# Four places of 4 MB for the expert weights, each matrix in two transfers

## The reference, cut to what matters

```
x = layer_norm(ALPHA * x + token_mixer(x), ln1_g, ln1_b)      # ends in merged @ w_out
logits = x @ router_w + router_b                              # 32 experts, top 4, softmax
for each expert e, for the tokens xb sent to it:
    gt = min(xb @ w_gate[e] + b_gate[e], 7)
    up = clip(xb @ w_up[e] + b_up[e], -7, 7)
    y  = (gt * sigmoid(1.702 * gt) * (up + 1)) @ w_down[e] + b_down[e]
out = layer_norm(ALPHA * x + sum of gate * y over a token's experts, ln2_g, ln2_b)
```

## Time and profile before

| | before |
|---|---|
| median of the runs | 2550.3 us |
| span of the profiled execution | 2550.5 us |
| TensorE busy | 2339.3 us (92%) |
| read from memory | 601.03 MB |
| transfers: queue of the kernel, share of 16 engines | 60.2% |

### The profile page before, as it was taken

The page is one execution under the profiler, slowest core; times in us unless marked ns, Lnnn a source line. Parts: engine busy times, 40 slices in busy tenths (PEclk is TensorE's granted clock), DMA queues, the critical chain, the costliest instruction groups (busy, mean ns, idle before and its releaser), DMA issues.

```text
span 2550.5 us, 32955 instructions
## 1 busy us (share of the span) xinstructions
PE 2339.3 (92%) x13502; PEld 1575.8 (62%) x13502; DVE 970.7 (38%) x1582; ACT 821.9 (32%) x1253; POOL 61.7 (2%) x34
## 2 busy tenths in 40 slices
PE   6989889999999977779999889999999999999996
PEld 4944777886888977679889788333333334333332
DVE  5466444343342486666654655211111111111112
ACT  4367433232242454635534673111111111111101
POOL 0000000000000023200000000000000000000000
PEclk8999999999999988889999999999999999999998
DMA  9287054432221300225546144999999999999995
GB/s 341 72 294 229 1 181 134 131 99 99 83 99 67 132 1 1 100 67 187 178 181 231 67 116 191 396 430 433 430 430 428 429 432 420 432 429 422 427 418 228
DMA packets 133298, 603.71 MB, mean 237 GB/s; under 512 B 5728, under 2 KB 51040, under 8 KB 116672
## 3 DMA queue, kind: packets, MB, share of 16 engines
q1 hardware_dynamic: 133184, 602.10, 60.2%
HBM read 601.03 MB, written 1.05 MB: 236 GB/s over the span
## 4 chain that ended last, share of the span: by engine, by line
PE 74%; DMA 11%; ACT 7%; DVE 5%; issue 2%; SPq 0%; ACTq 0%; DVEq 0%
PE bank L994 73%; DMA arena<-in_b_up 10%; ACT arena L1906 1%; DMA ring<-in_ada_w 1%; ACT modp L1681 1%; ACT w_high L2115 0%; ACT arena L2275 0%; ACT arena L2184 0%; ACT wide_p L2172 0%; ACT w_split L1747 0%; PE bank L1219 0%; PE bank L1589 0%; DVE arena L2745 0%; DVE last_sums L2684 0%; DMA ring<-in_ffn_w_up 0%
## 5 line engine op out<-in xcount | busy, mean ns | idle before, releaser
L994 PE MATMUL bank<-arena 128*64 128x512 f32 (+6 forms) x2264 | 447.2, 501 | 92.5 <-ACTq L782 29.0
L994 PEld LDWEIGHTS bank<-arena 128*64 128x64 f32 (+2 forms) x2264 | 207.3, 166 | 280.3 <-issue 194.1
L994 PE MATMUL bank<-hT_high,w_split 128*128 128x512 f32 (+1 forms) x1408 | 346.6, 337 | 2.5 <-DVE hT_low L2346 2.4
L994 PE MATMUL bank<-ring,arena 128*64 128x512 f32 (+1 forms) x1120 | 267.8, 593 | 2.1 <-ACT arena L2262 1.0
L994 PEld LDWEIGHTS bank<-hT_high,w_split 128*128 128x128 f32 x1408 | 242.1, 190 | 31.4 <-issue 2.8
L994 PE MATMUL bank<-up_w,arena 128*64 128x512 f32 x1024 | 233.6, 609 | 19.2 <-DMA arena<-in_b_up 19.1
L994 PE MATMUL bank<-hT_low,w_split 128*128 128x512 f32 (+1 forms) x704 | 236.6, 336 | 0.0
L3022 DVE TENSOR_SCALAR arena<-bank 128x512 f32<-128x512 f32 x32 | 22.1, 691 | 550.3 <-PE bank L994 550.0
L994 PEld LDWEIGHTS bank<-ring,arena 128*64 128x64 f32 (+1 forms) x1120 | 100.8, 141 | 162.7 <-issue 152.5
L994 PEld LDWEIGHTS bank<-up_w,arena 128*64 128x64 f32 x1024 | 78.8, 140 | 172.7 <-issue 172.7
L994 PEld LDWEIGHTS bank<-hT_low,w_split 128*128 128x128 f32 x704 | 133.6, 190 | 14.5 <-issue 1.0
(11 more groups left out here) (422 smaller groups left out, 4060.2 us busy)
## 6 DMA issues: line engine op xcount, KB each, us to landing
ring<-in_w_gate SPq DMA_DIRECT2D x32, 4096.0 KB
up_w<-in_w_up SPq DMA_DIRECT2D x32, 4096.0 KB
arena<-in_w_down SPq DMA_DIRECT2D x64, 2048.0 KB, 14.7
ring<-in_ada_w SPq DMA_DIRECT2D x24, 2048.0 KB, 8.7
ring<-in_ffn_w_up SPq DMA_DIRECT2D x44, 1024.0 KB, 7.7
ring<-in_w_in SPq DMA_DIRECT2D x11, 2048.0 KB, 8.0
ring<-in_ffn_w_down SPq DMA_DIRECT2D x10, 2048.0 KB, 7.7
ring<-in_hgrn_w_in SPq DMA_DIRECT2D x10, 2048.0 KB, 7.9
```

What stands on the lines that cost most here:

```text
L994: return pe.matmul(o, l, r, start=start, stop=stop)
```

## The change

- Four places of 4 MB: ring slots 1 and 2; the first two units of the arena; ring slot 0 with a further unit of the arena; and a new one over memory that is free after the router (half of `xr`, `hT`, half of `gb`). Matrix n goes to place n mod 4. The gate of expert e now waits for the down product of expert e-2 (gd_ready at e-1), the up for the gate product of expert e-1, the down for the up product of e-1.
- Each matrix goes as two transfers of 2 MB with a semaphore each for expert parity and half; TensorE waits for the second half only before k = 4. Gate and up halves are 16 KB out of every 32 KB for a partition.
- The first half of gate 0 is issued when ring slot 1 is free, the second at slot 2, up's halves after mixed_out(0,1) and (1,1), down 0 at once, gate 1 after the router's sums.
- Biases have two places. The bodies of TensorE's loop (two pairs) and SyncE's loop (four experts) are longer.
- The last `combine` stands ahead of the branch and closes the sums tile by tile; the further pass adds its own sums.
- The array `wide` is moved and worked in two halves.

```diff
-        moe_slot = [ring[:, i, :] for i in range(RING)] + [region(i * UNIT, UNIT) for i in range(6 - RING)]
+        freed_w = nc.alloc_sbuf_tensor_at("freed_w", [P, 2, UNIT], F32, offset=xr_at + 4 * XT * D)
+        moe_unit = [(ring[:, 1, :], ring[:, 2, :]), (region(0, UNIT), region(UNIT, UNIT)),
+                    (ring[:, 0, :], region(2 * UNIT, UNIT)), (freed_w[:, 0, :], freed_w[:, 1, :])]
+        WIDE = (ITEMS + 2) // 2
...
-        def expert_units(sp, e, i, first=False):
+        def expert_half(sp, name, e, buffer, j, landed):
+            w = a[name][0][bass.ds(e, 1)]
+            if name == "w_down_2":
+                src = w.rearrange("e (j p c) n -> p (e j) (c n)", j=2, p=P)[:, j, :]
+            else:
+                src = w.rearrange("e (p j c) n -> p (e j) (c n)", j=2, p=P)[:, j, :]
+            sp.dma_start(moe_unit[buffer][j], src).then_inc(landed[j], 16)
...
+        def first_experts(sp):
+            sp.wait_ge(SEM[owner[1][0]], owner[1][1])
+            expert_half(sp, "w_gate_2", 0, 0, 0, gate_landed[0])
+            expert_bias(sp, "b_gate_2", 0, 0, 0, gate_landed)
+            expert_bias(sp, "b_up_2", 0, 32, 0, up_landed)
+            sp.wait_ge(SEM[owner[2][0]], owner[2][1])
+            expert_half(sp, "w_gate_2", 0, 0, 1, gate_landed[0])
+            sp.wait_ge(psum_ready, group[("wo2", 0, 1)] + 1)
+            expert_half(sp, "w_up_2", 0, 1, 0, up_landed[0])
+            sp.wait_ge(psum_ready, group[("wo2", 1, 1)] + 1)
+            expert_half(sp, "w_up_2", 0, 1, 1, up_landed[0])
+            expert_weights(sp, "w_down_2", 0, 2, down_landed[0])
+            sp.wait_ge(psum_ready, group[("route",)] + 1)
+            expert_weights(sp, "w_gate_2", 1, 3, gate_landed[1])
...
+            sp.wait_ge(gg_ready, 1)
+            expert_weights(sp, "w_up_2", 1, 0, up_landed[1])
+            sp.wait_ge(gu_ready, 1)
+            expert_weights(sp, "w_down_2", 1, 1, down_landed[1])
+
+        def next_expert(sp, e, turn):
+            n = 3 * turn
+            sp.wait_ge(gd_ready, e - 1)
+            expert_weights(sp, "w_gate_2", e, n % 4, gate_landed[turn % 2])
+            expert_bias(sp, "b_gate_2", e, 0, turn % 2, gate_landed)
+            sp.wait_ge(gg_ready, e)
+            expert_weights(sp, "w_up_2", e, (n + 1) % 4, up_landed[turn % 2])
+            expert_bias(sp, "b_up_2", e, 32, turn % 2, up_landed)
+            sp.wait_ge(gu_ready, e)
+            expert_weights(sp, "w_down_2", e, (n + 2) % 4, down_landed[turn % 2])
...
             def projected(p, q, out, buffer, row, landed_sem, done):
                 for k in range(KC):
+                    if k % 4 == 0:
+                        pe.wait_ge(landed_sem[q][k // 4], (16, 32)[k // 4] * (p + 1))
...
-            with pe.Fori(1, E // 2 - 1) as p:
-                pair(p)
+            with pe.Fori(0, E // 4 - 1) as v:
+                for z in range(2):
+                    pair(2 * v + 1 + z, 1 + z)
             pe.wait_ge(rank_ready, 1)
             far_pairs = far_count(pe)
-            pair(E // 2 - 1, last=True)
+            pair(E // 2 - 1, E // 2 - 1, last=True)
             pe.wait_ge(yg_ready, E + 1)
+            combine(1, sums_closed)
...
             further(pe, far_pairs, far_pair)
-            combine(1, True).then_inc(sums_closed, 1)
...
-            dve.wait_ge(sums_closed, 1)
             for t in XS:
+                dve.wait_ge(sums_closed, t + 1)
                 for h in range(2):
                     mix(t, h, PS[4 + 2 * t + h])
```

More of the change, by code:

```diff
@@ L303, in program @@
         yg = region(M0 + 3584, 512)
-        bias = region(M0 + 4096, D)
+        bias = [region(M0 + 4096, D), last_e[:, :, :].rearrange("p a b -> p (a b)")]
         rw = region(M0 + 5120, KC, E)
@@ L751, in program @@
         ln_landed, rw_landed = sem("ln_landed"), sem("router_landed")
-        gate_landed, up_landed, down_landed = sem("moe_gate_landed"), sem("moe_up_landed"), sem("moe_down_landed")
+        gate_landed, up_landed, down_landed = ([[sem(f"moe_{kind}_landed_{parity}_{half}") for half in ("first", "second")]
+                                                for parity in ("even", "odd")] for kind in ("gate", "up", "down"))
         sel_ready, selg_ready, gx_ready, xg_ready, gt_ready, selgT_ready = (
@@ L803, in program @@
         block = ctx.enter_context(nc.Block())
-        def expert_units(sp, e, i, first=False):
[L808 to L823, removed]
-            for j in range(2):
[L825 to L839, removed]
@@ L858, in moe_sync @@
             sp.dma_start(rw[:, :, :], a["router_w_2"][0].rearrange("(k p) n -> p k n", p=P)).then_inc(rw_landed, 16)
-            expert_units(sp, 0, 0, first=True)
-            with sp.Fori(1, E) as e:
-                expert_units(sp, e, e)
+            first_experts(sp)
+            with sp.Fori(0, (E - 4) // 4) as v:
+                for z in range(4):
+                    next_expert(sp, 4 * v + 2 + z, 2 + z)
+            for e in range(E - 2, E):
+                next_expert(sp, e, e)
             sp.wait_ge(rank_ready, 1)
@@ L1564, in turn_sel, with combine @@
                 m.then_inc(gt_ready, 1)
-            def combine(q, last=False):
+            def combine(q, closed=None, opens=False):
                 for t in XS:
@@ L1608, in biases, with pair @@
                            False)
-            def pair(p, first=False, last=False):
-                i = 2 * p
+            def pair(p, turn, first=False, last=False):
+                i, n = 2 * p, 6 * turn
                 pe.wait_ge(xg_ready, 2 * (p + 1))
-                projected(i, 0, BG, 0, 0, gate_landed, gg_ready)
+                projected(p, 0, BG, n % 4, 0, gate_landed, gg_ready)
                 pe.wait_ge(yg_ready, i + 1)
-                projected(i, 0, BU, 2, 32, up_landed, gu_ready)
+                projected(p, 0, BU, (n + 1) % 4, 32, up_landed, gu_ready)
                 if first:
@@ L1632, in pair @@
                 turn_hidden(i + 1)
-                down(i + 1)
+                down(p, 1, (n + 1) % 4)
             keep_clock(SUM[1][1], 2)
@@ L1657, in far_pair @@
                     i = 2 * p + q + E
[L1658 to L1659 removed]
+                    projected(n, q, BG, 0, 0, gate_landed, gg_ready)
+                    projected(n, q, BU, 1, 32, up_landed, gu_ready)
                     if q:
                         pe.wait_ge(selgT_ready, n + 1)
[L1662 to L1663 removed]
+                        pe.wait_ge(far_taken, p + 1)
+                        combine(0, opens=True)
+                    else:
                         pe.wait_ge(selg_ready, 4 * (n + 1))
@@ L3077, in far_pair @@
                 n2 = E // 2 + p
-                link, n = chain(LINK0 + E // 2 * LINKS - 1 + p * 8)
+                link, n = chain(LINK0 + E // 2 * LINKS - 1 + p * 12)
+                dve.wait_ge(sums_closed, 2 * p + 2)
+                for t in XS:
+                    for h in range(2):
+                        o = xr[:, t, h * 512:(h + 1) * 512]
+                        link(STT(out=o, in0=PS[4 + 2 * t + h][:, :], scalar=1.0 / ALPHA, in1=o, op0=ALU.mult,
+                                 op1=ALU.add))
+                dve.sem_inc(far_taken, 1)
                 dve.wait_ge(gx_ready, n2)
```

72 lines of the change are left out of this document (42 added, 30 removed).

## The result

| | before | after |
|---|---|---|
| median of 4 runs side by side | 2549.55 us | 2533.18 us |
| ratio, 95% interval | | 0.9941 (0.9923 to 0.9959) |
| lowest and highest run | 2548.34, 2553.51 | 2532.31, 2539.79 |
| span of the profiled execution | 2550.5 us | 2530.5 us |

The kernel is faster by 0.6%; the medians lie 16.4 us apart. In a second comparison on one chip it was 2534.61 against 2550.84 us, ratio 0.9935 (0.9922 to 0.9948).

What follows compares the result with a forecast made beforehand. The prediction took the expert loop to be bound by weight transfers near 430 GB/s, with time to win only at its ends. Its terms: 2550.5 - 9.5 - 3.55 - 4.64 + 6.5 = 2539.3 us, taken as 2539; range 2530 to 2549.

Steps and rivals of the forecast that it cites:

- What bounds the kernel: Expert loop: claimed to go at the pace of weight transfers, DMA engines fully busy; time winnable only at the two ends.
- Start of the transfers: Start of the expert weights: early issues and a fourth place put the queue one matrix further, 9.87 us less 0.4 lost.
- rival 3: First expert pairs: slower TensorE lets the queue idle and the early matrix is given back, up to 2549 us; chance 0.06.
- Last matrices: Last up matrix: TensorE works on the first half while the second travels, -3.55 us; last down half stays hidden.
- Sum ahead of the branch: After the last expert: token sums run before TensorE's branch and close by tile, so VectorE's mixes start earlier, -4.64 us.
- Size of the pieces: Gates and ups in the loop: 16 KB instead of 32 KB a partition costs 0.11 us a matrix, +6.5 us.
- Rest: Remaining edits: waits per half, list arithmetic, second bias place, semaphores and longer bodies, claimed to cost nothing or at most 0.3 us.
- Rival 1: Split gates and ups: each added transfer costs a gap, slower above 0.28 us each, 2574 us at 0.65; chance 0.09.
- Rival 2: TensorE's longer loop body: instructions fetched anew each turn, 2541 us, or 2549 at 6 us a turn; chance 0.10.
- Rival 4: Last matrices: halves don't let TensorE start, or the last down half binds; 3.55 us lost, 2543 us; chance 0.05.

Runs made afterwards that it cites:

- the two table versions: Kernel after with all bias rows loaded once ahead of the experts, alone or also with whole-matrix transfers: 986.8 and 985.7 us from the router's weights issue to the end.

## Why the prediction held

Forecast 2539 in a range of 2530 to 2549; the median is 2533.2. The medians fell by 16.4 us where 11.3 was forecast (2550.3 to 2539). 3.0 us of that difference lie behind R, where the forecast comes to -17.7 + 6.5 = -11.2 and -14.2 was measured; for the other 2.1 no cause is shown. Point by point, for the stretch from R:

- **What bounds the kernel.** Right. The 100 us windows stay at 428 to 429 GB/s, and what moved the time was the start of the stream, the load or the pieces of its engines, or the tail behind it.
- **Start of the transfers, -9.5.** Right in its places and sizes. From R the steps should come at 0.0, 21.6, 81.3, 111.4 and 138.1 us (1541.6, 1563.2, 1622.89, 1652.93 and 1679.68 less 1541.56); they came at 0.4, 21.6, 81.4, 111.3 and 138.0. In R to R + 90 the kernel after moved 28.46 MB and the one before 24.27, 4.19 MB more: one matrix, 9.8 us. That it takes both the place and the early issue was the argument ("one matrix further", not 8 to 28 us), and the two experiments show it: the issues alone give 0, the place alone moves 25.99 MB in the first 90 us, 1.72 more than before or 4.0 us, and both together 5.8 us more. (Its last up landed 0.6 us later than before all the same: the pieces, below, took the 4.0 us back.) For gate 3, 0.4 us were forecast; the window 1640 to 1650 lost 0.2 us by its share of 0.98 and 0.7 by its 397 GB/s. After it no window of 100 us, up to 2500, has a share under 1.00 (rival 3).
- **Last matrices, -3.55.** Right. 11.62 to 7.99 us, -3.63. The last down half stayed hidden.
- **Sum ahead of the branch, -4.64.** Right. 6.77 to 1.85 us from the end of the down product to the first mix, -4.92; putting the sum behind the branch again, still tile by tile, costs 4.6.
- **Size of the pieces, +6.5: mis-sized.** The sign is right, 0.11 us a matrix is too much. The ends of the last waits of a pair lie 59.09 us apart before, (2512.05 - 1802.99) / 12 from the earlier trace rows, and 59.40 after: 0.31 for four gates and ups, 0.078 each, **+4.7 us** for 60. The experiment with whole matrices says 0.08. Also my 59.20 us a pair was taken from the starts of the pieces, which have nothing to do with landings; the ends are the measure, and they give 9.848 us a matrix. That alone would have placed gates at 9.85 and so no price below nothing. The mean also holds the bias rows, which was not seen: the two table versions, with none in the loop, give 58.73 / 6 = 9.79 us for a matrix in halves and (58.51 - 3 x 9.79) / 3 = 9.71 for a whole one, 0.08 less. The sum has a slip too: half way between 13.6 and -2 is 5.8, and 60 x 0.11 is 6.6, not 6.5.
- **Rest.** The terms as measured make -9.8 - 3.63 - 4.92 + 4.7 = -13.65, and 0.2 to 0.7 us less with the loss at gate 3; some 1 us is assigned to nothing. The remaining 5.7 us between the spans are the stretch ahead of R. It varies by 10.2 us over the runs above, whose edits don't touch it, so it is taken for chance; no run tests it.
- **Rivals.** Rival 1 wanted 0.28 us a transfer for a loss; with 0.078 for a matrix, which is one added transfer, it is out by a factor of 3.6. Rival 2: two instruction packets in 700 us, not one set for each turn. Rival 3: the windows from 1650 on stand at 1.00 or above. Rival 4: 7.99 us shows that TensorE starts on the half. The price of 2 us a transfer, which the Trainium skill gives (SBUF — State Buffer, section on the DMA setup-cost knee), is not seen between transfers that queue.

What the prediction did not see was larger than the 3.0 us that it was off behind R: the bias rows, which I costed at nothing "beside the same count of bias transfers". The change keeps their number, and in the kernel after they cost 7.9 us. In the kernel before no run leaves them out. Its last bytes show one engine late too, but by less (a share of 0.57 from 2515 to 2520 and 0.02 from 2520 to 2525), so what they cost there isn't shown.

## What to carry to other kernels

In a stream of transfers that sets the pace, a matrix has landed when the slowest DMA engine is done. Here a small transfer to a single partition was a load on one engine, and delayed the landings by about as much as sixteen times its bytes would. Load such rows once, as a table. An earlier issue is worth only as many bytes as there are places for, so count places and the release of the next one before counting microseconds; and take a period in a chain of waits from the ends of its pieces, not from their starts.

## What the hardware showed

- Bias rows of 4 KB: 0.17 us later landings for each, while the other engines go on (289.52 and 289.50 MB in 700 us, with and without rows). 62 of them are some 10 us on one engine; leaving out 60 gave 7.6 us, the table 7.9. The Trainium skill (DMA: Bandwidth & Descriptors, section "Why a DMA increments its semaphore by 16 and not by 1") says that a transfer is spread over the largest number of engines up to 16 that divides the slowest dimension longer than one of both its sides, on a hardware queue always the lowest-numbered ones. That all rows go through the same engine agrees with the window of 26 GB/s. The same section says that software can split a row so that it is spread; here the row in 16 pieces of 256 B was most likely spread, by its packets, and took 5.0 us more, so the measurement speaks against doing it.
- Two halves of 16 KB for a partition instead of 32 KB cost 0.07 to 0.08 us for 4.194 MB when they queue behind each other, with bias rows in the stream or without. Whether the added transfer or the smaller packets are the price, no run separates.
- A branch over an empty body cost TensorE 3.45, 3.49 and 3.88 us in the kernel before and two experiments (sum behind the branch, early issues alone), and the first 8 instructions behind it took 2.67, 3.70 and 3.15 us; the same 8 took 1.99 us ahead of the branch, in the kernel after. Each of the three stretches holds one or two packets of the instruction queue, which agrees with code being loaded there.
